# Attention probabilities normalised by a diagonal matrix inside their transposes

## The reference, cut to what matters

```
s = jnp.einsum('bhqd,bhkd->bhqk', qi, k).astype(jnp.float32)
s = jnp.where(key_pos[None, :] <= q_pos[:, None], s, -jnp.inf)
p = jax.nn.softmax(s, axis=-1)
return jnp.einsum('bhqk,bhkd->bhqd', p.astype(v.dtype), v)
```

## Time and profile before

| | |
|---|---|
| median of 3 runs | 3530.63 us (3529.11 to 3530.67) |
| the profiled execution, its own time | 3527.77 us |
| its span | 3526.1 us |
| TensorE busy | 3440.0 us, 98% of the span |
| VectorE busy | 2418.6 us, 69% |
| ScalarE busy | 1400.6 us, 40% |
| mean granted TensorE clock | 0.987 |
| attention of the first layer | about 226 to 356 us of the span |
| attention of the second layer | about 1966 to 2095 us |

### The profile page before, as it was taken

One profiled execution on the slowest core, in us unless ns is written; L12 is line 12 of the kernel. 1 busy time (PEld: TensorE's weight loads), 2 busy tenths in 40 slices (PEclk: granted clock), 3 DMA queues, 4 the chain that ended last, 5 costly groups with the idle time before them and its releaser, 6 DMA issues.

```text
span 3526.1 us, 53170 instructions
## 1 busy us (share of the span) xinstructions
PE 3440.0 (98%) x17910; PEld 2917.5 (83%) x17910; DVE 2418.6 (69%) x4725; ACT 1400.6 (40%) x2298; POOL 1374.1 (39%) x1287
## 2 busy tenths in 40 slices
PE   6999999999999999999989999999999999999998
PEld 5776789999999877777767777999999998777776
DVE  6455679999887865555454556799998868555554
ACT  3334344343576332222333343444346853323322
POOL 1010108666743424444300010277677325344442
PEclk9999999999999999999989999999999999999998
DMA  7554337776899989999764534577778999899995
GB/s 298 170 188 138 137 131 230 214 223 195 259 351 327 389 296 353 344 358 349 285 243 144 165 116 138 181 225 192 216 225 260 361 336 367 314 358 350 359 349 186
DMA packets 306402, 910.03 MB, mean 258 GB/s; under 512 B 69076, under 2 KB 101892, under 8 KB 305316
## 3 DMA queue, kind: packets, MB, share of 16 engines
q0 software_dynamic: 163216, 471.49, 39.0%
q1 hardware_dynamic: 106128, 385.92, 31.5%
q10 hardware_dynamic: 36868, 50.35, 3.9%
HBM read 792.14 MB, written 115.47 MB: 257 GB/s over the span
## 4 chain that ended last, share of the span: by engine, by line
PE 90%; DVE 4%; DMA 3%; issue 1%; ACT 1%; POOL 1%; SPq 0%; ACTq 0%; DVEq 0%; POOLq 0%
PE ps L457 15%; PE ps L459 14%; PE ps L458 14%; PE ps L1061 10%; PE ps L1063 10%; PE ps L1062 9%; PE ps L1075 3%; PE ps L1041 3%; PE ps L865 2%; DMA raw<-in_w_in 1%; PE ps L962 1%; PE ps L963 1%; PE ps L921 1%; PE ps L964 1%; PE ps L1001 1%
## 5 line engine op out<-in xcount | busy, mean ns | idle before, releaser
L457 PE MATMUL ps<-mov,whl 128*128 128x384 f32 (+1 forms) x2816 | 1008.2, 358 | 1.1 <-DVE whl L444 1.1
L459 PE MATMUL ps<-mov,whl 128*128 128x384 f32 (+1 forms) x2816 | 987.4, 351 | 0.0
L458 PE MATMUL ps<-mov,whl 128*128 128x384 f32 (+1 forms) x2816 | 986.8, 350 | 0.0
L444 DVE TENSOR_TENSOR whl<-raw,whl 128x1024 fp32r<-128x1024 f32 x648 | 793.5, 1225 | 240.7 <-ACT whl L434 236.1
L434 ACT CAST whl<-raw 128x1024 fp32r<-128x1024 f32 x648 | 679.6, 1049 | 149.2 <-ACT hst L1256 96.4
L1061 PE MATMUL ps<-whl,wgthl 128*128 128x512 f32 x1536 | 611.2, 398 | 2.3 <-DVE wgthl L1798 2.2
L1063 PE MATMUL ps<-whl,wgthl 128*128 128x512 f32 x1536 | 609.1, 397 | 0.0
L1062 PE MATMUL ps<-whl,wgthl 128*128 128x512 f32 x1536 | 603.8, 393 | 0.0
L457 PEld LDWEIGHTS ps<-mov,whl 128*128 128x128 f32 x2816 | 530.4, 188 | 39.6 <-issue 8.8
L459 PEld LDWEIGHTS ps<-mov,whl 128*128 128x128 f32 x2816 | 529.5, 188 | 31.7
L458 PEld LDWEIGHTS ps<-mov,whl 128*128 128x128 f32 x2816 | 530.3, 188 | 30.6 <-issue 2.4
(11 more groups left out here) (268 smaller groups left out, 3617.1 us busy)
## 6 DMA issues: line engine op xcount, KB each, us to landing
raw<-in_uT_tab SPq DMA_DIRECT2D x256, 512.0 KB, 4.4
raw<-in_v_tab SPq DMA_DIRECT2D x256, 512.0 KB, 6.7
expert_spill<-hst ACTq DMA_DIRECT2D x256, 192.0 KB
hin<-expert_spill POOLq DMA_DIRECT2D x256, 192.0 KB, 7.1
gt<-weight_spill POOLq DMA_DIRECT2D x64, 768.0 KB, 8.4
raw<-in_w_in SPq DMA_DIRECT2D x72, 512.0 KB, 4.8
raw<-in_w_mod SPq DMA_DIRECT2D x64, 512.0 KB, 3.7
weight_spill<-stage POOLq DMA_DIRECT2D x14, 2048.0 KB, 14.7
```

Of the source, the lines that this page charges most:

```text
L444: nc.vector.tensor_tensor(whl[:, m % RING, 1], raw[:, raw_n(m) % RAW], whl[:, m % RING, 0].bitcast(F32), ALU.subtract).then_inc(lo_done, 1)
L457: nc.tensor.matmul(o, w[:, 0, k], src[:, 0, k, :cols], start=(k == 0), stop=False)
L458: nc.tensor.matmul(o, w[:, 0, k], src[:, 1, k, :cols], start=False, stop=False)
L459: mm = nc.tensor.matmul(o, w[:, 1, k], src[:, 0, k, :cols], start=False, stop=(k == KC - 1))
```

## The change

VectorE no longer multiplies `pr`. It multiplies the identity, 128 by 128, by the reciprocals and so makes a diagonal matrix `share` for the unit; there are two such buffers. TensorE no longer uses its transpose with the identity, but a plain matmul of each block of `pr` with `share`, which gives the transposed block with every column scaled by the reciprocal of its row sum. Before it writes a buffer of `share` again, VectorE waits for the unit two before to have been transposed. The new buffers take the place in memory of part of `zp`, which is not used during attention.

```diff
@@ -292,6 +292,7 @@
     pr = sb("pr", [P, 2, S], at=pv_at)
     prT = sb("prT", [P, 4, S], at=lat_at)
     wpl = sb("wpl", [P, 2, 64])
+    share = sb("share", [P, 2, P], at=pv_at + 4 * TT * 2 * P)
     ht_at = top_of[0]
     ytmp = sb("ytmp", [P, 2, S])
     ht = sb("ht", [P, 2, S], at=ht_at)
@@ -928,8 +929,8 @@
                     pe.wait_ge(side_out, 1 + l * 12 + 12)
                     pe.wait_ge(prT_ready, 1 + l * 32 + max(i - 1, 0))
                     for j in range(t + 1):
-                        mm = nc.tensor.transpose(ps[:, 4 + i % 2, j * P:(j + 1) * P],
-                                                 pr[:, i % 2, j * P:(j + 1) * P], ident[:])
+                        mm = nc.tensor.matmul(ps[:, 4 + i % 2, j * P:(j + 1) * P], pr[:, i % 2, j * P:(j + 1) * P],
+                                              share[:, i % 2], start=True, stop=True)
                     mm.then_inc(pt_ready, 1)
                 elif kind == "pv":
                     two, t = divmod(i, TT)
@@ -1539,10 +1540,12 @@
                     nc.vector.tensor_scalar(nmx[:, b:b + 1], mx[:, b:b + 1], -SCALE, None, ALU.mult
                                             ).then_inc(max_ready, 1)
                 elif kind == "norm":
-                    n, b = (unit(i)[1] + 1) * P, i % 2
+                    b = i % 2
                     dve.wait_ge(exp_ready, 1 + l * 32 + i + 1)
+                    if i >= 2:
+                        dve.wait_ge(pt_ready, 1 + l * 32 + i - 1)
                     chain.link(nc.vector.reciprocal(rinv[:, b:b + 1], rsum[:, b:b + 1]))
-                    nc.vector.tensor_scalar(pr[:, b, :n], pr[:, b, :n], rinv[:, b:b + 1], None, ALU.mult
+                    nc.vector.tensor_scalar(share[:, b], ident[:], rinv[:, b:b + 1], None, ALU.mult
                                             ).then_inc(prob_ready, 1)
                 elif kind == "y":
                     k = Y_ORDER[i]
```

## The result

The changed kernel takes 3545.35 us (median of 9 runs, 3535.69 to 3550.41), the kernel before 3529.14 us beside it (9 runs, 3523.49 to 3530.67). The ratio is 1.0046, 95% interval 1.0037 to 1.0055: slower by 16 us. I had forecast 3546.2 us and +15.6. The sum came out; two of its terms did not, and they missed in opposite directions.

A forecast was written before the change was run, and what follows sets the result against it. TensorE, busy 98% of the span and 90% of the chain, was taken to bound the kernel. Attention's gapless stretch, +14.1 us, and its end, +1.5, made +15.6: 3530.63 to 3546.2 us, range 3538 to 3551.

The forecast's parts named there:

- the count of passes: Transposes at line 931: each plain float32 product takes two passes, 320 rows instead of 160.
- two regimes: Attention, per layer: 66 blocks while projection panels remain, TensorE always busy; then 14 blocks with gaps and a lower clock.
- the body's term: Attention while projection panels remain: a second pass of 0.107 us for 66 blocks in each of 2 layers, +14.1 us.
- My bound from the earlier trace: From line 923 to line 458's first matmul, with and without four transposes: 0.117 us more per block, 15.4 in all.
- VectorE in the tail: Attention behind the last panel: the shorter multiply gains 0.2 us once per layer, at the last unit only.
- The term of the tail: Attention behind the last panel: +0.65 us in the first layer and +0.9 in the second, +1.5 us.
- The last unit's four blocks run at the half clock: End of each layer's attention: four more passes of 0.213 us add 0.85 us.
- the rival that I had priced at -6.5 us: Behind the last panel: the clock stays at 2.4 GHz, total +7.6 us, 3538.2 us; chance 10%.
- My reason against this rival: Before line 962: TensorE has nothing during the last copy and rounding, and the change does not fill those; no size given.
- The new wait: VectorE's wait for the transposes of the unit two before: always met before it is asked, 0 us.
- The sum: Whole kernel: 14.1 + 1.5 = +15.6 us, 3546.2 us, 0.44% slower; chance 80%.

The follow-up runs named there:

- VectorE's half alone: Changed kernel with the transposes put back; VectorE makes the diagonal and nothing uses it: 3532.53 us beside 3531.32, ratio 0.9999.
- the change in the tail alone: Changed kernel with its new products and multiply only in units 28 to 31 of each layer, the rest as before: 3526.51 us beside 3531.32, ratio 0.9984.
- second profile of before: The kernel before, nothing changed, run and profiled once more to check its clock: 3525.17 us.

## Why the prediction was right, and where it was not

**What bounds the kernel, and the count of passes: right.** There are two regimes, and TensorE has no gap in the body; the new line has 320 rows; nothing covered the second pass. VectorE's half alone left the body as it was.

**The size of the body's term: too small.** The prediction put 66 blocks x 0.107 us per layer, 14.1 us together, with an upper bound of 15.4. The body grew by 16.7 us, outside the bounds. Two things were missing. The pass inside this stage costs 0.112 us, not the 0.107 us of line 888. And each unit loses, once, the 0.046 us by which its first transpose was cheaper, which neither line 888 nor line 1111 can show, since both are long runs of one kind. The price list gives for the body 8 x 0.158 + 8 x 0.268 + 6 x 0.385 + 6 x 0.499 = 8.7 us per layer; the last two blocks of the 66 lie behind the mark at unit 28, which takes off 0.27: 8.4, where 8.33 were measured. My bound from the earlier trace rows used the stage's own transposes, but put the pass of line 888 beside them; it mixed two places. It was also read from a unit with four blocks, where what is paid once is spread over four: by the price list the change adds 0.125 us a block there, but 0.158 in a unit with one. A body that grows by much more than 66 x 0.107 us was one of my signs of being wrong, and it came.

**VectorE in the tail: right in kind.** The chain there does not pass through the multiply except at the last unit. The gain is 0.2 to 0.3 us per layer. I had called all of TensorE's waits there longer than a microsecond; the one of unit 29 (344.80 in the trace before) was 0.50 us. It still covered that unit's three added passes.

**The term of the tail: wrong in sign.** The step that failed is "The last unit's four blocks run at the half clock". I carried the clock of the trace before over into the changed kernel, and counted +1.5 us. A full clock through the tail was one of my signs of being wrong. The clock held in the second layer and nearly in the first, and the tails got 3.7 us shorter. This is the rival that I had priced at -6.5 us for both layers and given 10%; where the clock holds fully in both, with the change in the tail alone, it is worth 5.3 us. Its price for the products behind attention was right: from line 962 to the merge that kernel takes 1.7 and 2.4 us less than before, just as counted. Its price for the last product was not: it counted 1.0 us in each layer, but up to line 962 all gains together, the shorter multiply's included, are 0.57 and 0.51 us. VectorE's timeline of the changed kernel shows why:

```profile
361.10 1.29 DVE L1553 TENSOR_TENSOR mov<-y,mov 128x512 fp32r<-128x512 f32 x2 [1.18 <-ACT mov L1230]
362.31 0.68 DVE L1558 COPY y<-ps 128x512 f32<-128x512 f32 x1
```

The last product ends at 361.7, but the copy of it starts only at 362.31, when VectorE has done its rest of `y`. The last product got 0.9 us shorter by the clock, but from its start to line 962 the way shrank from 3.12 to 2.71 us, by 0.4.

My reason against this rival was that TensorE has nothing to do during the last copy and rounding. That is still so (waits of 0.67 and 1.61 us), and yet in seven tails the clock stays up across them.

The rival's support in the Trainium skill, "TensorE: Matmul & The Clock Gate", Part 4, was that a transpose does not count as busy in the way a matmul does. The traces of this kernel disagree: doubled transposes hold the clock at 1.00 in both layers just as plain products do, and plain products in one pass lose it as single transposes do. The rival came true in the tail, but for another reason than the page's.

**The new wait: free, as said.** VectorE's half alone has it and its body is as before to 0.01 us.

**The sum: right partly by luck.** In the profiles +15.6 was forecast, and +16.7 - 3.7 in attention and +3.8 elsewhere were measured. The last number is scatter as far as these runs tell: the program outside the two attention stages took between 3248.9 and 3262.9 us over the ten profiled executions, with no order by kernel; the second profile of before has 3252.6 and the first 3254.5. Most of it in the changed kernel comes from one place in the first layer's expert stage, which I had expected to be as long as before (busy time by stretch again):

```profile
1288.00:1292.00 4.00, 4.00 (x13) 3.12 (x12) 3.03 (x5) 1.47 (x2) 0.54 (x1) 0.57 0.57 191
1284.00:1288.00 4.00, 1.84 (x8) 1.20 (x7) 1.75 (x3) 1.46 (x2) 0.54 (x1) 1.00 0.87 328
```

TensorE is busy for 1.84 of 4 us and then has the half clock, in code that is the same in both kernels. It waits for VectorE, and VectorE for the landing of a load; VectorE's timeline of the changed kernel, and at the same place of the kernel before:

```profile
1285.29 0.56 DVE L1789 TENSOR_TENSOR wgt<-hin,gt 128x384 f32<-128x384 f32 x1 [6.01 <-DMA hin<-expert_spill]
...
1276.37 0.56 DVE L1786 TENSOR_TENSOR wgt<-hin,gt 128x384 f32<-128x384 f32 x1 [4.07 <-DMA hin<-expert_spill]
```

Ahead of this place the changed kernel is 7.0 us later than the kernel before, and after it 10.5 us: that is 3.5 of the 3.8 us. Why the load landed later in this execution stays open.

## What to carry to other kernels

Folding a scaling into a transpose moves work from VectorE to TensorE, and in float32 it doubles TensorE's passes: where TensorE has no gaps, every pass is paid in full, and the relief of VectorE is worth nothing there. Price a pass inside the stage that it will stand in, at more than one group size, and look for a part that is paid once per group; long runs of one kind do not show it. Where TensorE works with gaps, its clock is part of the price: never carry the granted clock of one kernel over into a change of TensorE's work, and try filling the gaps near the end of such a stage, if need be with work that is thrown away.

## What the runs showed of the hardware that was not expected

- A float32 pass of 128 columns through 128 by 128 weights costs 0.111 to 0.114 us whether it is one of two passes of a plain product, the single pass in the rounded type, or a transpose; only the first transpose of a unit adds less, 0.064 us. The rounded type saves a pass, but makes none shorter at this size.
- Redundant TensorE work can shorten a kernel: 28 transposes made twice took the two tails from 48.52 us (47.77 in the second profile of before) to 43.51 us by keeping the clock at 2.4 GHz (ratio of the runs 0.9989, 0.9980 to 0.9999).
- In all ten tails with 14 passes the last product of a layer's attention ran at 1.2 GHz, in all ten with 22 or 28 at 2.4 GHz, whether the passes were transposes or plain products.
